# The weight ring of a decoder trunk as one array, 112 bytes further on

## The reference

```
x = x + 0.5 * rmsnorm(swiglu(rmsnorm(x), gate, up, down))    # FFN 1: 1024 -> 2816 -> 1024
x = x + rmsnorm(mixer(rmsnorm(x)))                          # RG-LRU and gated linear attention
x = x + 0.5 * rmsnorm(swiglu(rmsnorm(x), gate, up, down))    # FFN 2
swiglu(h) = (silu(h @ w_gate) * (h @ w_up)) @ w_down
mixer(h)  = concat(lru(h @ w_in), gla(h @ w_in)) @ w_out
```

## The kernel before

| array | offset mod 256 | used in |
|---|---|---|
| high rows of operand, hidden_pair | 0 | 514, streamed |
| low rows | 128 | 514, streamed |
| tiles of wh and wl | 0 | 514, loaded |
| top, low; ones | 128, 192; 64 | 757, 760, streamed; loaded |
| xc; gates | 0; 0 | 607, plain float32 |
| ident; values, keys | 192; 192, 0 | 683, 687, plain float32 |
| sc; vt | 64; 0 | 720, plain float32 |

## Time and profile before

### The profile page before, as it was taken

How to read it: one execution, slowest core, us unless ns; L and a number is a source line. 1 busy time by engine, 2 the same in 40 slices (tenths; PEclk the granted TensorE clock), 3 DMA queues, 4 the chain that set the end, 5 groups by cost and what they waited for, 6 DMA issues and landing times.

```text
span 2145.7 us, 41190 instructions
## 1 busy us (share of the span) xinstructions
PE 2137.5 (100%) x17197; PEld 2113.5 (98%) x17197; DVE 1440.6 (67%) x1902; ACT 1291.7 (60%) x1989; POOL 708.9 (33%) x708
## 2 busy tenths in 40 slices
PE   9999999999999999999999999999999999999999
PEld 9999999999999999999999999999999999999998
DVE  7555857678986658845584558577699867576454
ACT  7544657658785656653564456576578765575444
POOL 3112512525654225511240124124275533152112
PEclk9999999999999999999999999999999999999999
DMA  7555555445554455555555555554465545655553
GB/s 256 167 164 162 168 178 156 148 142 174 167 158 139 149 182 164 167 167 164 164 165 166 168 166 163 173 159 147 141 185 157 158 138 152 183 162 165 163 170 127
DMA packets 100551, 350.98 MB, mean 164 GB/s; under 512 B 11408, under 2 KB 12304, under 8 KB 100368
## 3 DMA queue, kind: packets, MB, share of 16 engines
q1 hardware_dynamic: 99936, 347.68, 53.0%
q10 hardware_dynamic: 432, 0.68, 0.1%
HBM read 343.45 MB, written 4.87 MB: 162 GB/s over the span
## 4 chain that ended last, share of the span: by engine, by line
PE 96%; DVE 1%; POOL 1%; issue 1%; DMA 0%; ACT 0%; SPq 0%; DVEq 0%; POOLq 0%; ACTq 0%
PE psD L514 92%; PE psM L607 1%; POOL ssum L1647 1%; PE psM L514 0%; DVE val L1503 0%; PE psM L648 0%; PE psM L720 0%; DVE wl L1178 0%; DMA x<-in_xT 0%; PE psM L683 0%; POOL hidden_pair L1848 0%; PE psS L534 0%; PE psM L727 0%; PE psD L500 0%; PE psM L587 0%
## 5 line engine op out<-in xcount | busy, mean ns | idle before, releaser
L514 PE MATMUL psD<-operand,wh 128*128 128x288 f32 x7328 | 1466.6, 296 | 0.9 <-DVE operand L1246 0.9
L514 PEld LDWEIGHTS psD<-operand,wh 128*128 128x128 f32 x7328 | 1174.0, 188 | 8.9 <-issue 4.7
L514 PE MATMUL psD<-operand,wl 128*128 128x288 f32 x3664 | 1076.3, 294 | 0.0
L1178 DVE TENSOR_TENSOR wl<-raw,wh 128x1024 fp32r<-128x1024 f32 (+2 forms) x656 | 822.5, 1255 | 109.5 <-ACT wh L834 109.1
L834 ACT ACTIVATE wh<-raw 128x1024 fp32r<-128x1024 f32 (+2 forms) x656 | 671.6, 1026 | 94.2 <-DMA raw<-in_w_gu 46.8
L514 PEld LDWEIGHTS psD<-operand,wl 128*128 128x128 f32 x3664 | 691.6, 189 | 0.0
L514 PE MATMUL psD<-hidden_pair,wh 128*128 128x288 f32 x2816 | 563.7, 296 | 0.6 <-POOL hidden_pair L1848 0.6
L1848 POOL TENSOR_TENSOR hidden_pair<-hid,hidden_pair 128x288 fp32r<-128x288 f32 x176 | 212.0, 1205 | 893.1 <-ACT hidden_pair L1122 893.1
L514 PEld LDWEIGHTS psD<-hidden_pair,wh 128*128 128x128 f32 x2816 | 450.4, 188 | 4.6 <-POOL hidden_pair L1848 3.1
L514 PE MATMUL psD<-hidden_pair,wl 128*128 128x288 f32 x1408 | 413.7, 294 | 0.0
L514 PEld LDWEIGHTS psD<-hidden_pair,wl 128*128 128x128 f32 x1408 | 265.7, 189 | 0.0
(11 more groups left out here) (246 smaller groups left out, 1362.9 us busy)
## 6 DMA issues: line engine op xcount, KB each, us to landing
raw<-in_w_gu SPq DMA_DIRECT2D x351, 512.0 KB, 3.6
raw<-in_w_d SPq DMA_DIRECT2D x128, 448.0 KB, 3.3
raw<-in_w_in SPq DMA_DIRECT2D x80, 512.0 KB, 3.5
raw<-in_w_d SPq DMA_DIRECT2D x64, 512.0 KB, 3.6
raw<-in_w_out SPq DMA_DIRECT2D x32, 512.0 KB, 3.5
x<-in_xT SPq DMA_DIRECT2D x8, 288.0 KB, 7.1
gates<-in_w_ax SPq DMA_DIRECT2D x4, 512.0 KB, 4.4
S<-in_st_gla SPq DMA_DIRECT2D x4, 512.0 KB, 4.5
```

The lines of the kernel that those rows point to most:

```text
L514: mm = e.matmul(out, w[:, kt * P:(kt + 1) * P], t[:, kt, :], start=(kt == 0 and part == 0), stop=(kt == KT - 1 and part == 2))
L1178: e.tensor_tensor(wl[u % RING][:, part], raw[u % RING][:, part], wh[u % RING][:, part].bitcast(F32), ALU.subtract).then_inc(lo_ready, 1)
```

## The change

The twelve slots become one array `ring` with a lead of LEAD = 28 words (112 bytes) ahead of the first slot and 4 words (16 bytes) behind the last; `raw_ring` is the same bytes typed float32. `wh`, `wl` and `raw` become slices of them. All tiles of the ring move up by 112 bytes, everything behind the ring by 128 bytes. Modulo 256, a high row then begins 144 bytes past the beginning of a tile and a low row 16 bytes past it, where before it was 0 and 128. No instruction is added, removed or reordered.

```diff
+LEAD = 28
...
-    wh = [sb(f"wh{s}", [P, D], F32R) for s in range(RING)]
-    raw_at = cursor[0]
-    raw = [sb(f"raw{s}", [P, D]) for s in range(RING)]
-    cursor[0] = raw_at
-    wl = [sb(f"wl{s}", [P, D], F32R) for s in range(RING)]
+    ring_at = cursor[0]
+    ring = sb("ring", [P, LEAD + 2 * RING * D + 4], F32R)
+    ring_end = cursor[0]
+    cursor[0] = ring_at
+    raw_ring = sb("raw_ring", [P, LEAD + 2 * RING * D + 4])
+    assert cursor[0] == ring_end
+    wh = [ring[:, LEAD + s * D:LEAD + (s + 1) * D] for s in range(RING)]
+    wl = [ring[:, LEAD + s * D:LEAD + (s + 1) * D] for s in range(RING, 2 * RING)]
+    raw = [raw_ring[:, LEAD + s * D:LEAD + (s + 1) * D] for s in range(RING, 2 * RING)]
```

## The result

The changed kernel takes 2124.15 us (median, 2122.97 to 2124.8) against 2147.2 us before: a ratio of 0.989, 95% interval 0.9873 to 0.9907, 23 us faster. The forecast was "no change", at 2146.9 us, and is wrong; the rival "the new relation is better" (2113 to 2147 us, middle 2130) is what happened. A second measurement of the same kernel gave 2123.86 us, ratio 0.989 (0.9877 to 0.9904).

A forecast was written before the change was run, and what follows sets the result against it. TensorE's start-to-start pace bounds the kernel: 15,360 loop matmuls at 132.3 ns, 2032 us of the 2145.7 us span. All terms summed to 0, so the forecast was the unchanged median, 2146.9 us, range 2113 to 2181.

The forecast's parts named there:

- the new relation is better: Rival, loop matmuls: part of the 12.3 ns above the columns is a collision; 2113 us far end, 2130 middle; chance 0.33.
- The first reading: 512-column sums pay 21.7 ns above columns, 288-column loop matmuls 12.3; surplus grows with width, leaving 0.2 to 3.4 ns for collisions.
- The second reading: Plain float32 matmuls: 2.5 ns surplus at 288 columns; 64 bytes off may be dearer by 1.3 to 3.0 ns, 2.2 taken.
- The direct term: Ring tiles moved by 112 bytes: 15,360 loop matmuls times d, the change in ns per matmul; d forecast 0, ends 34 us either way.
- Behind the ring: Gate, sums, ones and mixer arrays move by 128 bytes; a few dozen loads and rows, at most 0.1 us, taken as 0.
- splits: ScalarE's copy and VectorE's subtraction per weight unit, now 16 bytes off a 32-byte boundary; covered by TensorE, cost 0.
- landings: DMAs into the ring, now 16 off a multiple of 32; 182 to 364 ns a packet, costing nothing up to 1.89 times.
- The rival of doubled packets: Queue of 656 ring transfers: packets at 16 off a 32-byte boundary cost double, 364 ns, giving 2274 us; chance 0.05.
- The 3% of additional beats: Ring DMA packets: 132 beats become 136 by the page's counting, an estimated 188 ns a packet; no term in the sum.
- The read ports: TensorE: rows and weight load have their own read ports, so the load takes no bandwidth; would make the change exactly 0.
- The other rival: New relation is worse: load and row meet in memory at every loop matmul; up to 2181 us, middle 2164; chance 0.20.
- unchanged: The forecast's own case: the relation moves but neither side reads memory in a way that knows it; 2146.9 us, chance 0.42.

The follow-up runs named there:

- the blocks with one row for all tiles: Kernel before with 288-column matmuls appended behind its last one, one streamed row, sixteen tile distances of 0 to 240 bytes; no distance below 131.1 ns a matmul.
- the blocks of 512 columns: Kernel before with 512-column matmuls appended, distances 0, 16, 32, 64, 112, 240 bytes: 226.7 ns at 0, 16 and 240, 233.3 at 32, 64 and 112.
- the tables: Kernel before with blocks of matmuls appended behind its last one at many row-to-tile distances; the loop's pattern took 132.2 ns at 0 bytes, 130.0 at 112.
- the pair before: Kernel before with blocks appended, high tile 0 and low tile 128 bytes off their rows, entered 25 ways: 132.2 ns a matmul in all 25 blocks.

## Why the prediction was wrong, point by point

**The bound** was read rightly: TensorE's own pace decides, no wait does. Everything that the change did to the time is in the pace of the loop's matmuls.

**The first reading** is the step that failed. The prediction compared 288 columns at distances 0 and 128 with 512 columns at 64 off, found 9.4 ns more surplus, laid it to the streamed width, and so had at most 3.4 ns left for a collision. Two things had changed at once, and the blocks with one row for all tiles take them apart. Between 0 and 64 off the distance alone is worth 13.3 - 11.7 = 1.6 ns at 288 columns; from 288 to 512 columns the width alone is worth 13.4 - 11.7 = 1.7 ns at distance 0; both together are worth 20.0 - 11.7 = 8.3 ns. The remaining 1.1 ns is the rounding of two steps of 0.23 us, less 0.6 ns that the loop pays above the block with one row. So the premise that a collision costs the same at both widths is wrong: between 0 and 64 off it is 1.6 ns at 288 columns and 6.6 ns at 512. The prediction had even noted the 64 off, and took it as evidence that the distance is immaterial. Without this reading, nothing stood against a collision in the 12.3 ns. The first of the two sums itself loads its next tile at 192 off, a distance that the blocks of 512 columns don't have; its starts in the trace of the kernel before are 231 to 234 ns apart in the four cases without a stop, close to the slower pace.

**The second reading** was right in what it took for itself, that 64 off might be dearer by 1.3 to 3 ns, and the 2.2 ns drawn from it came near the size of the better rival: the fast units moved by 132.3 - 129.9 = 2.4 ns. That was luck, as plain matmuls can't say what a load costs the float32r stream. Nor is a row always one matmul: lines 607 and 720 have two rows for each matmul that they issue, so a plain matmul of 288 columns takes 485 ns and pays 5 ns above 480. As 128 float32r columns already take 111.8 ns with a load each, the load in the loop may well lie beside nearly the whole stream of 120 ns; no run shows the two apart.

**The direct term** d = 0 was mis-sized: d was -2.4 ns in 309 units, -1.1 in 343, -1.73 on the mean. The mixture is why the result, 2124, lies between the far end of the rival (2113) and its middle (2130); at 129.9 ns throughout it would be an estimated 2110.

**Behind the ring, splits, landings**: all three at 0, and right. The 272 bytes that the lead of 256 moves them are worth 1.0002; the splits grew by 2 ns and 1 ns; the landings stayed at 3.6 us. The rival of doubled packets is out. The 3% of additional beats that the Trainium skill's page "DMA: Bandwidth & Descriptors" (section "How a descriptor splits into AXI transactions") would give is not seen: the packets' time is 53.7% of 2121.8 us against 53.0% of 2145.7, 0.2% more. In the second profile of the changed kernel it is 54.1%, 0.9% more, so two profiles of one kernel differ by more than the first difference.

**The read ports.** That weight loads take nothing from the stream whatever the relation, which the prediction cited from the Trainium skill's page "TensorE: Matmul & The Clock Gate" (section "Step-by-step: what each phase is for"), doesn't hold for this float32r loop: with the same instructions, and with all other engines idle (the tables), the distance of the tile to the row moves the pace between 129.9 and 135.6 ns. The measurement decides; how the load reaches the stream, no run shows.

**The other rival**, a worse relation, was sized at up to +34 us; a lead of 16 bytes shows +45. The range of the prediction was wide enough for the change that was made, but not for others of its kind. **The chances** gave better 0.33 and unchanged 0.42. Since every row the trace offered stood at a multiple of 64, no reading could carry "unchanged"; the open question deserved the larger part.

## What to carry to other kernels

Where TensorE is never idle and its matmuls still take 10% longer than their columns, the places of the streamed rows and of the tiles loaded beside them, modulo 256 bytes, are worth a table: append blocks of the loop's own pattern at all distances behind the kernel, read the start distances, and check the winner and a loser in the kernel itself. Blocks must be long (the pair before needed dozens of matmuls to settle) and entered in several ways. Compare two rows of a trace only where one thing differs: a row that differed in width and distance told about neither.

## What the runs showed of the hardware that I had not expected

- The pace of a float32r matmul of 288 columns with a load each depends on the two distances, 129.9 to 135.6 ns, the same after a shift of 256 bytes (a lead of 256 bytes: ratio 1.0002), not additive over the loads, and sensitive to 4 bytes.
- What a distance costs depends on the width: between 0 and 64 bytes off 288 columns (one row for all tiles) lose 1.6 ns and 512 columns 6.6 ns.
- Rows and tiles moved together by an odd multiple of 16 bytes cost 133.3 ns where even multiples give 130.0 or 131.1.
- One and the same pair has two lasting paces (130.0 and 131.1 ns), picked by how the stream is entered. In the kernel they can last over whole stages, and 556 of 656 units had the same one in two executions.
- Float32r matmuls of 128 columns with a load each come every 111.8 ns, at all six distances tried.
- That the two streams are read from the same part of the memory and stop each other fits all of this, but no run shows the mechanism: it is argued, not shown.
